# Gate and up projections of a SwiGLU block with the weights as the stationary operand

## The reference

```
def rmsnorm(x, g):
    y = xf * lax.rsqrt(jnp.mean(xf * xf, axis=-1, keepdims=True) + EPS)
    return (y * g).astype(x.dtype)
def swiglu(x, w_gu, w_down):
    gate, up = jnp.split(x @ w_gu, 2, axis=-1)
    return (jax.nn.silu(gate) * up) @ w_down
h = h + 0.5 * swiglu(rmsnorm(h, ffn1_norm), ffn1_w_gu, ffn1_w_down)
h = h + hybrid_mixer(rmsnorm(h, mix_norm), ...)
h = h + 0.5 * swiglu(rmsnorm(h, ffn2_norm), ffn2_w_gu, ffn2_w_down)
h = h + sigmoid(rmsnorm(h, ple_norm) @ w_ple_gate) * (p @ w_ple_proj)
out = rmsnorm(h, final_norm)
```

## Time and profile before

| | us |
|---|---|
| Time, median of 3 runs | 548.53 (547.25 to 548.68) |
| The profiled execution's own time | 547.51 |
| Its span on the core | 545.7 |

### The profile page before, as it was taken

One profiled execution on the slowest core, in us unless ns is written; L12 is line 12 of the kernel. 1 busy time (PEld: TensorE's weight loads), 2 busy tenths in 40 slices (PEclk: granted clock), 3 DMA queues, 4 the chain that ended last, 5 costly groups with the idle time before them and its releaser, 6 DMA issues.

```text
span 545.7 us, 6911 instructions
## 1 busy us (share of the span) xinstructions
PE 535.4 (98%) x2583; PEld 435.5 (80%) x2583; DVE 311.9 (57%) x375; ACT 272.2 (50%) x333; POOL 11.9 (2%) x24
## 2 busy tenths in 40 slices
PE   8999999999999999999999999999999999999994
PEld 4888888888788888877777888888888888888883
DVE  4675555455534554456798685555555654353575
ACT  5955354443525364875153764534435343343746
POOL 1400000000000010000000000000000000000000
PEclk9999999999999999999999999999999999999998
DMA  8996556563577467431246285665655536427202
GB/s 300 376 328 208 173 179 205 160 209 131 185 246 266 156 239 243 127 125 58 78 156 210 75 297 171 191 194 165 212 161 190 195 130 214 170 102 232 77 1 77
DMA packets 72549, 98.37 MB, mean 180 GB/s; under 512 B 3376, under 2 KB 48640, under 8 KB 72400
## 3 DMA queue, kind: packets, MB, share of 16 engines
q1 hardware_dynamic: 71104, 93.34, 51.7%
q0 software_dynamic: 1264, 4.68, 2.5%
q10 hardware_dynamic: 160, 0.07, 0.1%
HBM read 97.01 MB, written 2.63 MB: 183 GB/s over the span
## 4 chain that ended last, share of the span: by engine, by line
PE 94%; DVE 3%; DMA 1%; issue 1%; ACT 0%; DVEq 0%
PE acc L482 86%; PE turn L524 4%; PE side L482 3%; DVE w_lo L1098 1%; DMA h<-in_x 1%; DVE AT L1329 1%; PE turn L482 0%; ACT L1068 0%; DVE E L1219 0%; DVE pr L1274 0%; DVE pr L1275 0%; DVE prT L1282 0%; DVE AT L1315 0%; DVE E L1218 0%; DVE oT_lo L1309 0%
## 5 line engine op out<-in xcount | busy, mean ns | idle before, releaser
L1098 DVE TENSOR_TENSOR w_lo<-raw,w_hi 128x2048 fp32r<-128x2048 f32 (+1 forms) x89 | 197.2, 2219 | 107.0 <-ACT w_hi L836 106.9
L482 PE MATMUL acc<-w_hi,hT_hi 128*128 128x512 f32 x496 | 197.8, 399 | 0.0
L482 PE MATMUL acc<-w_hi,hT_lo 128*128 128x512 f32 x496 | 193.6, 390 | 0.0
L482 PE MATMUL acc<-w_lo,hT_hi 128*128 128x512 f32 x496 | 193.3, 390 | 0.0
L836 ACT ACTIVATE w_hi<-raw 128x2048 fp32r<-128x2048 f32 (+1 forms) x89 | 164.8, 1856 | 55.5 <-PE acc L482 54.9
L482 PEld LDWEIGHTS acc<-w_hi,hT_hi 128*128 128x128 f32 x496 | 93.2, 188 | 20.6 <-issue 2.2
L482 PEld LDWEIGHTS acc<-w_hi,hT_lo 128*128 128x128 f32 x496 | 93.1, 188 | 20.1
L482 PEld LDWEIGHTS acc<-w_lo,hT_hi 128*128 128x128 f32 x496 | 93.3, 188 | 18.0
L482 PE MATMUL acc<-w_hi,a_hiT 128*128 128x512 f32 x176 | 69.1, 392 | 0.0
L482 PE MATMUL acc<-w_hi,a_loT 128*128 128x512 f32 x176 | 68.5, 389 | 0.0
L482 PE MATMUL acc<-w_lo,a_hiT 128*128 128x512 f32 x176 | 68.5, 389 | 0.0
(11 more groups left out here) (165 smaller groups left out, 313.6 us busy)
## 6 DMA issues: line engine op xcount, KB each, us to landing
raw<-in_ffn_w_gu SPq DMA_DIRECT2D x86, 512.0 KB, 4.5
raw<-in_ffn_w_down SPq DMA_DIRECT2D x40, 512.0 KB, 4.6
raw<-in_w_in SPq DMA_DIRECT2D x24, 512.0 KB, 4.4
raw<-in_w_out SPq DMA_DIRECT2D x8, 512.0 KB, 4.2
raw<-in_w_ple_gate SPq DMA_DIRECT2D x8, 512.0 KB, 4.2
raw<-in_ffn_w_down SPq DMA_DIRECT2D x8, 256.0 KB, 3.0
bias_skew_dram<-bias_row_dram POOLq DMA_DIRECT2D x1, 1536.0 KB, 8.2
h<-in_x SPq DMA_DIRECT2D x2, 512.0 KB, 5.2
```

Of the source, the lines that this page charges most:

```text
L482: return nc.tensor.matmul(o, lhsT, rhs, start=start, stop=stop, skip_group_check=True)
L1098: V.tensor_tensor(w_lo[:, slot, :nk * N], raw[:, slot, :nk * N], w_hi[:, slot, :nk * N].bitcast(F32), ALU.subtract).then_inc(lo_ready, 1)
```

## The change

The stationary operand of the gate and up product becomes the weight tile (128 rows x 128 columns), and the moving one the turned activation. `hT_hi` and `hT_lo` of a chunk now lie side by side in one tile `hT`, so that `w_hi` meets both in one matmul of 512 columns, and `w_lo` meets `hT_hi` in one of 256. The result comes transposed: 128 weight columns on the partitions, tokens along the free dimension. The left 256 columns of a bank hold two of the three products, the right 256 the third, and they must be added up. A block's four column groups (two of gate, two of up) take one bank each, all four banks, group after group, each through all 8 chunks.

- `act_turn` goes, on TensorE, ScalarE and VectorE, with its 4 transposes for each block.
- ScalarE, in each block: copy the right halves of the gate banks, silu (in place, from SBUF), copy the right halves of the up banks, split of one unit, copy to `a_hiT`, split of the other unit. VectorE, in each block: add the left gate halves, multiply by the row scale, add the left up halves, multiply gate by up, split, `a_loT`, split.
- The row scale now varies along the free dimension. `spread` (VectorE) and `r_turn` (two transposes on TensorE, after the first column group of block 1; a copy on VectorE) make `r_rows`, once for each feed-forward block. Only the gate is scaled before silu. The up half's scale is applied behind the second stage: `resid` multiplies by `rhalf`, half of `rstd`, in place of 0.5.
- The next block's first gate group waits until the gate banks of this one are read, and its first up group until the up banks are. Both units of a block must be split before the block begins, and both slots come free at its end.
- At the kernel's start split 3 moves ahead of the squares and the root on ScalarE, and ahead of `rms(0)` on VectorE. In the second feed-forward block VectorE's and ScalarE's first split of the next units moves behind `gated`.

The core of the diff (constants for counters and the tile declarations cut):

```diff
-            def act_turn(f, b, par):
...
-            def gu_block(f, b, par, s0, first=False):
...
+            def gu_cols(g, slot, kh, ks=range(CH)):
+                for k in ks:
+                    c = CH * kh + k
+                    w = slice(k * N + g * P, k * N + (g + 1) * P)
+                    mm(acc[:, g, 0:T], w_lo[:, slot, w], hT_hi[:, c, :], c == 0, False)
+                    ins = mm(acc[:, g, :], w_hi[:, slot, w], hT[:, c, :, :].rearrange("p a t -> p (a t)"), False, c == KC - 1)
+                return ins
...
+            def gu_block(f, b, s0):
+                pe.wait_ge(lo_ready, b * 2 + (U_GU[f] + 2))
+                for g in range(4):
+                    if g == 0:
+                        pe.wait_ge(acc_read, b * 4 + (2 * B_GU[f] - 2))
+                    elif g == 2:
+                        pe.wait_ge(acc_read, b * 4 + 2 * B_GU[f])
+                    for kh in range(2):
+                        ins = gu_cols(g, (s0 + kh) % RING, kh)
+                    if g == 1:
+                        ins.then_inc(gate_done, 1)
+                    if g == 0 and isinstance(b, int) and b == 1:
+                        r_turn(f)
+                ins.then_inc(unit_done, 2)
...
+                    act_e.wait_ge(gate_done, b + (NB * f + 1))
+                    A(silu_g[:], acc[:, 0:2, T:N], ACT.Copy).then_inc(g_part, 1)
+                    act_e.wait_ge(g_scaled, b + (NB * f + 1))
+                    A(silu_g[:], silu_g[:], ACT.Silu).then_inc(silu_ready, 1)
+                    act_e.wait_ge(unit_done, b * 2 + (U + 2))
+                    if f or j:
+                        act_e.wait_ge(a_lo_ready, b + NB * f)
+                    A(act[:], acc[:, 2:4, T:N], ACT.Copy).then_inc(u_part, 1)
+                    sp_(0)
+                    act_e.wait_ge(act_ready, b + (NB * f + 1))
+                    A(a_hiT[:, bass.ds(b * 2, 2), :], act[:], ACT.Copy).then_inc(a_hi_ready, 1)
                     sp_(1)
...
+            def gated(f, b):
+                dve.wait_ge(g_part, b + (NB * f + 1))
+                V.tensor_tensor(silu_g[:], acc[:, 0:2, 0:T], silu_g[:], ALU.add).then_inc(acc_read, 2)
+                dve.wait_ge(acc_read, b * 4 + (2 * B_GU[f] + 2))
+                if isinstance(b, int) and b == 0:
+                    r_turn(f)
+                V.tensor_tensor(silu_g[:], silu_g[:], view(r_rows[:], [[0, 2], [1, T]]), ALU.mult).then_inc(g_scaled, 1)
+                dve.wait_ge(u_part, b + (NB * f + 1))
+                V.tensor_tensor(act[:], acc[:, 2:4, 0:T], act[:], ALU.add).then_inc(acc_read, 2)
...
-            rms(0)
             split(3)
+            rms(0)
+            spread(0)
```

More of the change, by code:

```diff
@@ L58 @@
 UNITS = 90
[L59 to L65, removed]
+B_GU = [0, 32]
+B_DOWN = [22, 54]
+B_WIN = 24
+B_WOUT = 30
+B_PROJ = 56
+B_GATE = 58
+B_H = {1: 22, 2: 30, 3: 54}
 MIX = {
@@ L146, in plan_turns @@
     add("h2.1", 2)
-    add("act1", NB)
     add("p")
@@ new lines, in r_turn, with gu_first @@
+            def r_turn(f):
+                o = side_open(f"r{f}")
+                pe.wait_ge(r_spread, f + 1)
+                for m in range(M):
+                    ins = flip(o[:, m * P:(m + 1) * P], r_cols[:, m, :])
+                ins.then_inc(side_done, 1)
+            def gu_first(f):
+                u, s, B = U_GU[f], 2 * f, B_GU[f]
+                acc_free(B)
+                if f == 0:
+                    pe.wait_ge(half_lo, 1)
+                    h_turns(s, 1)
+                    h_ready(s, 0, 0)
+                    for g in range(4):
+                        gu_cols(g, u % RING, 0, range(2))
+                    pe.wait_ge(lo_ready, 1)
+                    h_ready(s, 0)
+                    for g in range(4):
+                        ins = gu_cols(g, u % RING, 0, range(2, CH))
+                else:
+                    pe.wait_ge(lo_ready, u + 1)
+                    h_ready(s, 0)
+                    for g in range(2):
+                        gu_cols(g, u % RING, 0)
+                    h_turns(s, 1)
+                    acc_free(B + 1)
+                    for g in range(2, 4):
+                        ins = gu_cols(g, u % RING, 0)
+                ins.then_inc(unit_done, 1)
+                pe.wait_ge(lo_ready, u + 2)
+                h_ready(s, 1)
+                for g in range(2):
+                    ins = gu_cols(g, (u + 1) % RING, 1)
+                ins.then_inc(gate_done, 1)
+                for g in range(2, 4):
+                    ins = gu_cols(g, (u + 1) % RING, 1)
+                ins.then_inc(unit_done, 1)
@@ L862, in root @@
                 A(rtmp[:, s, :], rtmp[:, s, :], ACT.Sqrt).then_inc(root_ready, 1)
[L864 to L880, removed]
             def ffn(f):
@@ L1017, in _ @@
             split(2)
+            split(3)
             squares(0, 0)
@@ L1130, in rms, with spread @@
                 dve.wait_ge(rstd_ready, s + 1)
-            def act_turn(f, b, par):
-                dve.wait_ge(turn_hi, b + (hi_count[f"act{f}"] + 1))
-                r = bass.ds(b * 2, 2)
[L1135 to L1143, removed]
+            def spread(f):
+                for m in range(M):
+                    ins = V.tensor_scalar(r_cols[:, m, :], ident[:], 0.0, rstd[:, 2 * f, m:m + 1], ALU.mult, ALU.add)
+                ins.then_inc(r_spread, 1)
+                V.tensor_scalar(rhalf[:, f, :], rstd[:, 2 * f, :], 0.5, None, ALU.mult)
@@ L1145, in ffn, with act_low @@
+            def act_low(f, b):
+                dve.wait_ge(a_hi_ready, b + (NB * f + 1))
+                r = bass.ds(b * 2, 2)
+                V.tensor_tensor(a_loT[:, r, :], act[:], a_hiT[:, r, :].bitcast(F32), ALU.subtract).then_inc(a_lo_ready, 1)
             def ffn(f):
@@ L1157, in blk @@
                             rms(2)
-                            sp_(0)
-                    else:
-                        act_turn(f, b - 1, (j - 1) % 2)
-                        sp_(0)
-                    gated(f, b, j % 2)
-                    if f == 0 and j == 0:
-                        sp_(0)
+                            spread(1)
+                    gated(f, b)
+                    sp_(0)
+                    act_low(f, b)
                     sp_(1)
```

103 lines of the change are left out of this document (41 added, 62 removed).

## The result

| | before | after |
|---|---|---|
| Time, median (all runs), us | 548.03 (547.25 to 549.38) | 552.62 (549.05 to 555.64) |
| The profiled execution's own time, us | 547.51 | 554.21 |
| Its span, us | 545.7 | 552.4 |

The change makes the kernel 0.8% slower: ratio 1.008, 95% interval 1.0067 to 1.0093. I had forecast 550.8 us in a range of 546.9 to 554.3. Beside the 4.6 us, the spread tells something: the kernel before keeps within 2.1 us, the changed one takes 6.6.

What follows compares the result with a forecast made beforehand. TensorE's instruction stream was taken to bound the kernel. Stream -5.3, row-scale transposes +0.6, first start +5.1 and second +2.0 made +2.4 us on the median's footing of 548.53, given as 550.8 us, range 546.9 to 554.3.

Steps and rivals of the forecast that it cites:

- The first gap: First feed-forward block, between blocks 0 and 1: TensorE waits 3.2 us for VectorE's gate add.
- The four later stalls: Behind block 0 of both feed-forward blocks: TensorE waits 0.8 and 1.25 us, then 0.75 and 1.25 us.
- The clock: Rival: clock falls in the gap at the first feed-forward block's start, adding 2.8 us, giving 553.6; chance 0.20.
- The stream: Gate and up matmuls of 22 blocks: 11.12 us each, activation transposes gone, net -5.3 us.
- The sum: Whole kernel: -5.3 + 0.6 + 5.1 + 2.0 = +2.4 us.
- Stalls and transposes: Starts of the two feed-forward blocks: waits cost +5.1 and +2.0 us, the row scale's added transposes +0.6 us.
- the clock's case: Rival: half-speed matmuls behind the first feed-forward block's gap, around 553.6 us; chance 0.20.
- The steady state's cover: Steady gate and up blocks: VectorE finishes 2.5 us before TensorE needs its results, so nothing waits.

Runs made afterwards that it cites:

- early_gate: The changed kernel with the copy and add of block 0's gate halves moved ahead of squares, root and spreading at the kernel's start; 548.53 us, ratio 1.0009.
- r_early: The changed kernel with the second feed-forward block's two row-scale transposes issued in block 0, behind the gate groups, instead of block 1; 552.57 us.

## Why the prediction was right, and where not

The direction and the mechanism stand: TensorE's stream gets a little shorter, and the stalls at the two starts take back more.

- *The first gap.* Forecast at 22.8 us, 3.2 us long, ended by the gate add behind root and spreading. It came at 23.1, 2.5 us long, by just that chain. Split 3 waited for its unit until 17.73 (I had 17.7), the reciprocal ended at 24.3 (24.3), the resume came at 25.63 (25.95): I counted the small operations without their overlap and the hop to TensorE too long (0.15 us from the add's end at 25.48, not 0.27). The other half of the difference is block 0, which ended 0.3 us later. `early_gate` shows that it was the order.
- *The four later stalls.* Forecast 0.8, 1.25, 0.75, 1.25; measured 0.6, 1.1, 0.6, 1.2, each ended by the add that I had named. `r_early` removes the last two.
- *The clock.* I gave its fall in the gap 0.20. By the mean clocks it falls in most executions. The row I had for it said so: at the kernel's end the clock fell 2.7 us after the last matmul, I forecast a gap of 3.2, and I still called it the less likely case. The price is 1.6 us in the profile, not 2.8: 3.4 us at half speed, which began 0.6 us after TensorE had gone on. The Trainium skill ("TensorE: Matmul & The Clock Gate", "Why this matters for your kernels") warns of idle gaps between bursts of matmuls; those it warns of are longer than the ones measured here, which brought the clock down at 2.05 us of idle time and not at 1.72.
- *The stream.* This is the term that was mis-sized. I added the price of a long matmul among long ones to that of a short one among short ones: 0.3475 us. Of the 16 feed-forward blocks profiled in alternating order, 7 run their steady blocks at that (0.3467, 11.09 us) and 9 at 0.353. That is 11.21 us for a block on average, 2.0 us more over 22 blocks. The loads, listed with 0.19 us, hide under the short matmul's 0.117 in both. The Trainium skill ("TensorE: Matmul & The Clock Gate", "LDWEIGHTS (loading the stationary operand)") gives them an estimated 107 ns, and the trace agrees. The trace before held a hint, of one matmul: behind the last row, the first long matmul after the short ones, the next one in the kernel before is this:

```profile
210.00 0.39 PE L482 MATMUL acc<-w_lo,hT_hi 128*128 128x512 f32 x1
```

  From 209.76 that is 0.24 us, not 0.2275. A change of length may have had its price there, and I never looked for it.
- *The sum.* Forecast +2.4. Stalls and transposes 1.4 less, low clock 1.6 more, pitch 2.0 more: +4.6; measured +4.6. Two errors of the same sign, one of the other; the range held since it reached to the clock's case. That the terms meet the measured figure to a tenth is luck: the low clock isn't in every execution, and 2.0 is an average over profiles of several kernels. (The forecast's own sum, 548.53 + 2.4, is 550.9, not 550.8.)
- *The steady state's cover.* 2.5 us forecast. VectorE's gate add ends at 71.54 in the changed kernel, for a block that begins about 74.5. It held.

## What to carry to other kernels

When a change lets the next step reuse the bank that the last one is still read from, look at the first turn of the loop, where set-up work stands on the reading engine: put the read that frees the bank ahead of all set-up that the bank doesn't need. A gap of 2.5 us cost 4.0 here by the timelines, since the clock fell behind it; the same move, with the other stalls out, turned a change that lost 0.8% into one that wins 0.4%. Where a kernel's runs spread wider than its parent's, compare the lengths of steady loops in several executions before a median of few runs is believed.

## What the hardware showed that I had not expected

A strictly alternating stream of 256- and 512-column matmuls, each with its own load, has two speeds: 0.347 and 0.353 us for a pair, held as long as the stream is unbroken (up to 328 pairs) and open again behind each wait or inserted instruction, at a full granted clock and with TensorE waiting for nobody in between. Equal lengths (0.120 us each) and runs of two or eight (11.145 and 11.17 us for a block) showed one in the one or two profiles of each. After a gap of 2.5 us the clock went to its half level only once TensorE was at work again, at 26.2 us, and stayed there for 3.4 us.
